# Squaring the first half of every token tile behind its own addition, ahead of the second norm

## The reference

```
h  = rms_norm(x, norm_mix);  proj = h @ w_in
x  = x + concat(retention, forgetting attention, short conv) @ w_out
h2 = rms_norm(x, norm_ffn)                       # "the second norm"
x  = x + (silu(dwconv3(h2 @ w_gate)) * (h2 @ w_up)) @ w_down

rms_norm(x, g) = x * rsqrt(mean(x*x) + 1e-6) * g
```

## Time and profile before

| | us |
|---|---|
| median of three runs | 1549.01 |
| profiled execution | 1548.17 |
| its span (first to last instruction) | 1546.1 |
| TensorE busy | 1530.9 (99%) |
| VectorE busy | 1053.9 (68%) |
| ScalarE busy | 662.2 (43%) |
| GpSimd busy | 414.8 (27%) |
| second norm of layer 0, of layer 1 | 328 to 351, 1100 to 1123 |

### The profile page before, as it was taken

The page is one execution under the profiler, slowest core; times in us unless marked ns, Lnnn a source line. Parts: engine busy times, 40 slices in busy tenths (PEclk is TensorE's granted clock), DMA queues, the critical chain, the costliest instruction groups (busy, mean ns, idle before and its releaser), DMA issues.

```text
span 1546.1 us, 28264 instructions
## 1 busy us (share of the span) xinstructions
PE 1530.9 (99%) x9827; PEld 1337.3 (86%) x9827; DVE 1053.9 (68%) x1804; ACT 662.2 (43%) x1233; POOL 414.8 (27%) x526
## 2 busy tenths in 40 slices
PE   9999999999999999999999999999999999999998
PEld 7878886789999999999878789867899999999997
DVE  3555367459977787888645553674599888888885
ACT  4323347236544444444332233472465444444441
POOL 1214120014533333333012130100144333333330
PEclk9999999999999999999999999999999999999999
DMA  9224546522322222222332325465223222222222
GB/s 318 69 71 95 174 157 230 182 69 83 95 82 81 81 81 81 81 81 68 111 93 57 85 69 184 156 232 178 64 83 95 82 81 81 81 81 81 81 69 86
DMA packets 118361, 166.75 MB, mean 108 GB/s; under 512 B 28800, under 2 KB 81024, under 8 KB 114192
## 3 DMA queue, kind: packets, MB, share of 16 engines
q1 hardware_dynamic: 117856, 165.18, 34.0%
q10 hardware_dynamic: 432, 0.59, 0.1%
HBM read 155.86 MB, written 9.63 MB: 107 GB/s over the span
## 4 chain that ended last, share of the span: by engine, by line
PE 92%; DVE 3%; SPq 1%; DMA 1%; ACT 1%; issue 1%; POOL 0%; DVEq 0%; POOLq 0%; ACTq 0%
PE bank L2348 89%; PE bank L2410 3%; DMA raw<-in_w_in 1%; DVE pf L1993 1%; DVE pf L2006 0%; SPq L718 0%; DVE xn L1647 0%; SPq L815 0%; DMA raw<-in_w_gate 0%; DVE gulo L1629 0%; DVE x L2123 0%; POOL small L1008 0%; ACT xn L1260 0%; SPq L735 0%; DVEq L2137 0%
## 5 line engine op out<-in xcount | busy, mean ns | idle before, releaser
L2348 PE MATMUL bank<-whi,hhi 128*128 128x512 f32 x560 | 223.7, 402 | 1.7 <-ACT hhi L1275 1.2
L2348 PE MATMUL bank<-whi,hlo 128*128 128x512 f32 x560 | 217.5, 391 | 0.0
L2348 PE MATMUL bank<-wlo,hhi 128*128 128x512 f32 x560 | 216.9, 390 | 0.0
L2348 PE MATMUL bank<-hhi,whi 128*128 128x320 f32 x640 | 198.7, 310 | 0.8 <-DVE hlo L1629 0.8
L2348 PE MATMUL bank<-hhi,wlo 128*128 128x320 f32 x640 | 197.8, 309 | 0.0
L2348 PE MATMUL bank<-hlo,whi 128*128 128x320 f32 x640 | 197.6, 309 | 0.0
L2348 PE MATMUL bank<-whi,guhi 128*128 128x512 f32 x440 | 171.9, 391 | 0.2
L2348 PE MATMUL bank<-wlo,guhi 128*128 128x512 f32 x440 | 171.3, 389 | 0.0
L2348 PE MATMUL bank<-whi,gulo 128*128 128x512 f32 x440 | 171.3, 389 | 0.0
L1605 DVE TENSOR_TENSOR wlo<-raw,whi 128x1024 fp32r<-128x1024 f32 x79 | 100.1, 1266 | 95.8 <-ACT whi L1191 94.4
L2123 DVE TENSOR_TENSOR x<-x,bank 128x512 f32<-128x512 f32 x220 | 142.7, 680 | 29.4 <-PE bank L2348 28.9
(11 more groups left out here) (323 smaller groups left out, 3567.1 us busy)
## 6 DMA issues: line engine op xcount, KB each, us to landing
raw<-in_w_in SPq DMA_DIRECT2D x51, 512.0 KB, 4.0
raw<-in_w_gate SPq DMA_DIRECT2D x44, 512.0 KB, 3.8
raw<-in_w_down SPq DMA_DIRECT2D x44, 512.0 KB, 3.6
raw<-in_w_up SPq DMA_DIRECT2D x24, 512.0 KB, 3.8
vb<-in_cache_fox_v SPq DMA_DIRECT2D x10, 1024.0 KB, 5.8
gains<-in_w_up SPq DMA_DIRECT2D x20, 512.0 KB, 3.8
raw<-in_w_out SPq DMA_DIRECT2D x16, 512.0 KB, 5.3
bcr<-scr_p SPq DMA_DIRECT2D x8, 512.0 KB, 5.4
```

The source lines that it names most:

```text
L2348: return pe.matmul(out, lhsT=lhsT, rhs=rhs, start=start, stop=stop, skip_group_check=True)
```

## The change: what it does

```diff
-        small = own("small", [P, 544])
+        small = own("small", [P, 560])
+        HSS, HVAR = 544, 552
+        half_sq = sem("half_sq")
 # GpSimd, norm(which, l)
+                if which == 1:
+                    pool.wait_ge(half_sq, l * TT + TT)
+                    apart(pool)
+                    pool.tensor_scalar(col(HVAR, TT), col(HSS, TT), 1.0 / D, EPS, ALU.mult, ALU.add)
+                    pool.drain()
                 for t in range(TT):
                     pool.wait_ge(sumsq, l * (2 * TT) + which * TT + t + 1)
                     apart(pool)
-                    rsqrt(SS + t, VAR + t, RS + t, 1, 1.0 / D, rstd)
+                    rsqrt(SS + t, VAR + t, RS + t, 1, 1.0 / D, rstd, EPS if which == 0 else col(HVAR + t))
 # ScalarE, norm(which, l, splits)
-                        act.activation(xn[:, t % 2, :], x[:, t, :], ACT.Square, accum_out=col(SS + t)).then_inc(sumsq, 1)
+                        c0 = 512 * which
+                        act.activation(xn[:, t % 2, c0:], x[:, t, c0:], ACT.Square, accum_out=col(SS + t)).then_inc(sumsq, 1)
 # ScalarE, ahead of the second norm
+                upto(WO + 6, l)
+                for t in range(TT):
+                    B.wait_taken(act, ("wo", 0, t), l)
+                    if t >= 2:
+                        act.drain()
+                    act.activation(xn[:, t % 2, 0:512], x[:, t, 0:512], ACT.Square, accum_out=col(HSS + t)).then_inc(half_sq, 1)
                 upto(G0 - 1, l)
+                act.drain()
                 norm(1, l, {0: G0, 3: G0 + 1, 4: G0 + 2})
```

## The result

The changed kernel takes 1555.67 us (median of six runs, 1555.13 to 1556.15) against 1548.84 us of the kernel before (six runs, 1547.78 to 1549.34). The ratio is 1.0045, with a 95% interval of 1.0035 to 1.0055: 6.8 us slower, where 0.9 us faster was forecast. The profiled execution took 1555.13 us, its span is 1552.8 us against 1546.1.

What follows compares the result with a forecast made beforehand. TensorE, 99% busy, was taken to bound the kernel, so only its gaps around the second norms could give time: 0.55 + 0.38 = 0.93 us off the median of 1549.01 gave 1548.1 us, range 1546.2 to 1549.8 us.

Steps and rivals of the forecast that it cites:

- the sum: Tile 4's earlier start on TensorE in both layers' second norms, added up: 0.55 + 0.38 = 0.93 us gained.
- The slower rival: Feed-forward loop: shifted phase brings TensorE's 0.40 us wait for ScalarE's copy into 19 other passes, 1555.7 us; chance 0.05.
- The square, 0.63 us: ScalarE in the second norm: each square takes 0.63 us instead of 1.06, so 0.43 us shorter.
- The prepared column, +0.07 us: GpSimd's scalar operation in the norm: adding a column instead of a constant costs 0.07 us more per tile.
- The added squares: ScalarE ahead of the norm: five squares end by some 316.3 us, before `WO + 7`'s split, 1.6 us room, no cost.
- Tile 3: Second norm: VectorE's multiply, and the transposes after it, come 0.36 us earlier in layer 0 and 0.20 in layer 1.
- TensorE's gap at the gate product: Second norm, TensorE: the idle time ahead of the gate product, 0.41 us in layer 0, stays unchanged.
- Tile 4 and the port: Second norm: VectorE's split lengthens GpSimd's scalar operation to about 0.4 us; TensorE gets tile 4 0.55 and 0.38 us earlier.
- the port does not bite: Second norm, tile 4: GpSimd's scalar operation runs beside VectorE's split, so 1.28 us gained, 1547.7 us; chance 0.15.
- GpSimd gets in front of VectorE: Second norm, tile 1: GpSimd's scalar operation starts first and delays VectorE's split; 0.64 us gained, 1548.4 us; chance 0.15.
- Nothing arrives: Behind the norm a wait takes the gain, or the half squares save too little: zero, 1549.0 us; chance 0.13.
- The forecast for the norm: Second norm: TensorE has tile 4 earlier by 0.55 us in layer 0 and 0.38 us in layer 1.

Runs made afterwards that it cites:

- with the change in place: The changed kernel with `small` back at 544 columns and the new columns in unused ones, so no address differs from the kernel before: 1547.6 us, ratio 0.9996.
- With the change and 256 bytes: The changed kernel with `small` 608 columns wide, everything behind it 256 bytes further than in the kernel before: 1547.83 us, ratio 0.9997.

## Why the prediction was wrong

**The failed step is the sum.** It added up instructions, waits and queues, and left out the one line of the diff that has none of them, the width of `small`. The prediction said "No DMA is moved" and, of GpSimd's new operation, "Its cost is nothing too", and never asked what the declaration moves: 64 bytes in front of two tensors that are the stationary operand of 1320 matmuls. The missing term is +7.7 us, eight times the forecast gain.

**The slower rival gave the right number by chance.** "The loop falls into another step" came to 1555.7 us, and the passes did become 0.36 us longer. But its cause was a wait in every pass for ScalarE's copy, brought on by the phase. The trace has no such wait in the passes, and with the change in place, where order and instructions are those of the changed kernel, the passes take 38.33 us. So it was refuted. Of this rival only the first pass of a layer is left. With the change in place TensorE waits there for ScalarE's copy of `gu` 0.42 us in layer 0 and 0.35 us in layer 1:

```profile
1178.96 0.41 PE L2363 MATMUL bank<-t3h,xhi 128*128 128x320 f32 x1 [0.35 <-ACT gu L1543]
```

**The square, 0.63 us:** right, 0.633 us over ten. **The prepared column, +0.07 us:** right, L1008 takes 0.27 us where nothing is in its way. **The added squares:** right. They run from 311.72 to 316.1 us, and the split of `WO + 7` starts at 317.55 us with 1.46 us of room left, against the 1.6 estimated (the split itself lies 0.36 us earlier than in the earlier trace rows, and so do the transposes of tile 0, by 0.37 us: this execution was ahead before the norm began).

**Tile 3:** right in kind, undersized: its transposes come 0.51 and 0.30 us earlier after tile 0's (8.54 us in both layers, 9.05 and 8.84 before), not 0.36 and 0.20. VectorE now multiplies it without idle time, as forecast, but a multiply that need not wait starts 0.08 us ahead of the recorded end of the remainder before it (339.52 against 338.32 + 1.28 = 339.60), and I had let it start behind. In layer 0 the power also lost the 0.36 us that it had waited for nothing visible. One sign failed: TensorE's gap at the gate product was to stay and grew from 0.41 to 0.56 us in layer 0 (0.44 to 0.56 in layer 1). The gate product waits for VectorE's remainder of tile 2, and this came only 0.36 us earlier after tile 0's transposes, not 0.51: the remainder also needs ScalarE's rounding of tile 2, which follows that tile's transposes and so didn't move (7.92 us after tile 0's transposes, 7.89 before).

**Tile 4 and the port:** right in mechanism. This is GpSimd and VectorE in the changed kernel, layer 0, from the timeline of all engines:

```profile
342.88 1.23 DVE L1620 TENSOR_TENSOR wlo<-raw,whi 128x1024 fp32r<-128x1024 f32 x1
...
343.75 0.48 POOL L1008 TENSOR_SCALAR small<-small 128x1 f32<-128x1 f32 x1 [4.29 <-ACT xn L1268]
344.38 0.55 POOL L1010 TENSOR_TENSOR small<-small,mhalf 128x1 f32<-128x1 f32 x1
...
344.97 1.29 DVE L1662 SCALAR_TENSOR_TENSOR xn<-x,small,gains 128x1024 f32<-128x1024 f32 x1 [0.86 <-POOL small L1010]
```

L1008 is held until VectorE's split ends at 344.11, and ends 0.12 us behind it: 0.48 us in place of 0.27. So tile 4's chain lost about 0.2 us of its saving, and the rival "the port does not bite" falls. So does "GpSimd gets in front of VectorE": in tile 1 L1008 started at 331.49, within the multiply of tile 0, and took 1.67 us; it was held through the multiply and through the split that followed at 331.89 without delay:

```profile
330.69 1.28 DVE L1662 SCALAR_TENSOR_TENSOR xn<-x,small,gains 128x1024 f32<-128x1024 f32 x1 [0.21 <-issue]
...
331.49 1.67 POOL L1008 TENSOR_SCALAR small<-small 128x1 f32<-128x1 f32 x1 [1.74 <-ACT xn L1268]
331.89 1.22 DVE L1620 TENSOR_TENSOR wlo<-raw,whi 128x1024 fp32r<-128x1024 f32 x1
```

"Nothing arrives" is not separated by the timing, whose interval holds zero and the forecast. In the trace most of the norm's gain reaches the first down product: from tile 0's transposes to it there were 53.01 us in layer 0 and 52.53 in layer 1, and with the change in place there are 52.49 and 52.25, that is 0.52 and 0.28 us less. Then layer 1's first pass took 38.88 us against 38.26 before, with the wait shown above, and in that execution layer 1's gain was gone. With the change and 256 bytes the same pass took 38.26 us and the gain stayed; and the kernel before with `guhi` alone moved has a long first pass in layer 1 as well (39.00 us against 38.51 later). So the runs do not tell whether the change brings that wait about.

**The forecast for the norm** was 0.55 and 0.38 us; with the change in place it is 14.58 - 13.97 = 0.61 and 14.37 - 13.97 = 0.40. That it is so close is in part luck. In the changed kernel the multiply of tile 4 came 0.47 and 0.26 us earlier after tile 0's transposes, less than forecast, while its transposes now start 0.05 us behind the recorded end of the multiply, where it was 0.16 before (344.97 + 1.29 = 346.26 against 346.31; 345.81 + 1.29 = 347.10 against 347.26).

## What to carry to other kernels

Read a declaration in a diff as you read an instruction: list which tensors it moves and which matmuls read them. For matmuls like these, of 512 columns, keep the stationary and the moving operand, and the stationary tensors used in turn, at the same place modulo 256 bytes, or put the new columns where nothing moves. And when busy time grows with the count of instructions unchanged, compare the mean duration by form first: there is no wait to look for.

## What the runs showed of the hardware

- In the down product, matmuls of 512 columns (f32 in the rows, declared float32r) step every 0.227 us when all their operands lie at distances of a multiple of 256 bytes, and every 0.233 us with both stationary tensors 32 or 64 bytes off, at the full granted clock. At 128 bytes the mean step was 0.232 us, at 192 bytes 0.229 us.
- Such matmuls of 320 columns showed no such effect at any placement tried: means of 0.144 to 0.150 us a step, 306 to 312 ns in the rows.
- The weight load's own rows did not change (PEld, the engine of these loads, is busy 1337.3 us before and 1337.5 after the change); the time appears only in the matmuls.
- A GpSimd operation of 0.27 us on `small`, asked for during a VectorE multiply that was followed at once by a split, took 1.67 us and ended 0.05 us behind the split (333.16 against 331.89 + 1.22 = 333.11); the split was not held up.
